# Latent streams of a two-block transformer kernel: a first pass for eight picks, and tile 1's heads between the first value sums

## The chip, the cores and the metric

The kernel runs on one core of one Trainium2 chip. The metric is the device time of one execution in microseconds (us). Before the change it is 2879.14 us, the median of three executions (2868.58 to 2879.42).

## The reference, cut to what matters

Two blocks of two layers each run over 256 positions with 1024 channels, all in float32. The change touches the second block's latent layers. Such a layer mixes (attention with 8 heads over 512 keys, beside a convolution) and then applies `peer`, which picks 16 of 16384 experts per head and position:

```
q = (h @ w_pq).reshape(B, T, PEER_HEADS, 2, PEER_HALF)            # 8 heads, 2 halves
s = jnp.einsum('bthcd,hckd->bthck', q, sub_keys)                  # 128 keys per half
top_s, top_i = lax.top_k(s, PEER_TOPK)                            # 16 of 128, per half
cand = top_s[..., 0, :, None] + top_s[..., 1, None, :]            # 16 x 16 sums
best_s, best_j = lax.top_k(cand.reshape(..., 256), PEER_TOPK)     # 16 of 256
expert = top_i[0][best_j // 16] * PEER_KEYS + top_i[1][best_j % 16]
w = softmax(best_s)
act = gelu(einsum('cd,ced->ce', h, u_tab[expert]))
out = einsum('ce,ced->cd', act * w, v_tab[expert])
```

Each position has its own 128 experts (8 heads of 16), and each expert is one row of u and one of v, 8 KB together.

## The kernel before, in words

The 256 positions are two tiles of 128, one position per partition. The context part and the first block run first, then the two latent layers, one after the other. A latent layer ends in a stream of 256 fetches: fetch n brings, for each of the 128 positions of tile n // 128, the u and v of that position's pick n % 128, which is 1 MB (an indirect DMA that GpSimd issues in `latent_pool`, L2950). Every fetch then goes through four steps in order of n: VectorE multiplies u with h and sums (the dot, L2895); ScalarE takes the gelu (L2835), multiplies with the weight (L2838) and scales an identity by it (L2842); TensorE multiplies that with v and sums over all picks of the tile in PSUM (the value sum, L2756).

The data lands in slots of 8 KB per partition. `ring_plan` gives each fetch the slot that has been unused longest among those that `SLOT_FROM_TO` allows for its n. A slot that has been used waits for the value sum of its last fetch; a slot that is taken for the first time waits for whatever held its memory. `SLOT_QKT` lies on the attention's queries and keys, `SLOT_PROBS` on its probabilities, `SLOT_W0A` and `SLOT_W1A` (from n = 24) on weights that tile 1's last product reads.

The order on each engine is written out by hand. The other work of the layer is hung between the fetches: `latent_mixer_pe`, `latent_mixer_act` and `latent_mixer_dve` each return a table from n to a step. TensorE and ScalarE run the step of n before their part of fetch n, VectorE runs it after the dot of n, and after it the search step of `SEARCH_AT`. A search is `search_keys` (two rounds of eight maxima with their indices over 128 keys, for two halves) and `search_pairs` (the same over 256 sums, then the indices through one-hot sums). The picks of head h are fetches 16 h to 16 h + 15 of their tile; heads 0 and 1 have key scores of their own, and the searches of heads 1, 2 and 3 are hung at n = 1 and 4, 8 and 14, 21 and 27.

Tile 1's attention heads (QH = 8 to 15) have these pieces: a score on TensorE (L802), its maximum on VectorE (L1476), the exponentials on ScalarE (`exps`, L1132), the transposition on TensorE (`turn_probs`, L820), its copy on ScalarE (`probs_turned`, L1140) and the product with the values on TensorE (`sum_values`, L829); at the end `merge_heads` on VectorE (L1498). Before the change TensorE and ScalarE do all of this ahead of fetch 0; VectorE takes two maxima at -2 and two at -1, then two after the dots of 0 and 1, and merges after the dot of 2.

## Time and profile before

| what | value |
|---|---|
| median of three executions | 2879.14 us |
| the profiled execution's own time | 2881.62 us |
| its span, first to last instruction | 2879.7 us |
| TensorE, VectorE, ScalarE, GpSimd busy | 84%, 73%, 28%, 38% of the span |
| 1038.87 MB by DMA, over the span | 361 GB/s |
| dots L2895, mean | 1219 ns |
| value sums L2756 in W slots, mean of one matmul | 627 ns |
| idle before the dots in W slots | 188.1 us, for a DMA |

The profiled execution lies 2.5 us above the median, 1.9 us of it outside the span. The two latent streams lie at about 1393 to 2069 us and 2208 to 2871 us of the span. Busy shares are means over stages with different limits, so the rows further below are of one stage.

### The profile page before, as it was taken

What the parts mean: (1) busy time and instruction counts of PE and PEld (TensorE: products, weight loads), DVE (VectorE), ACT (ScalarE), POOL (GpSimd) and SP (SyncE); (2) the same over time, 40 slices, a digit from 0 to 9 for tenths busy, and PEclk for the clock granted to TensorE, in tenths of its full rate; (3) what the DMA queues carried; (4) which work ended last, traced back from release to release, by engine and by line L of the source; (5) the groups of instructions that cost most, each with busy time, mean ns of one, the idle gap of its engine ahead of it and who ended that gap; (6) DMA issues with size and microseconds to landing.
All of it is one profiled execution on the core that took longest, in us unless ns stands there. A gap on an engine that the chain in (4) does not pass through costs nothing.

```text
span 2879.7 us, 27669 instructions
## 1 busy us (share of the span) xinstructions
PE 2409.2 (84%) x8548; PEld 1374.1 (48%) x8548; DVE 2108.8 (73%) x4518; ACT 816.6 (28%) x2272; POOL 1100.1 (38%) x1090
## 2 busy tenths in 40 slices
PE   6886887989987899988798877869797998877876
PEld 3654464756546566656444333324374444332322
DVE  1869479888878978868787777765475877777654
ACT  1221111000102100013443443334324544433443
POOL 0000444856463676532243333334121434333331
PEclk9897987999986899998999899899998999998999
DMA  8548999999999999963699999999933999999997
GB/s 334 225 164 334 399 413 376 368 412 412 393 407 381 384 398 412 412 259 104 265 398 420 415 420 420 420 419 404 372 124 119 382 420 421 420 421 420 420 420 320
DMA packets 183477, 1038.87 MB, mean 361 GB/s; under 512 B 26971, under 2 KB 28978, under 8 KB 99876
## 3 DMA queue, kind: packets, MB, share of 16 engines
q0 software_dynamic: 147456, 805.37, 69.2%
q1 hardware_dynamic: 35292, 230.38, 20.0%
q8 instruction: 69, 1.13, 0.2%
q10 hardware_dynamic: 584, 1.36, 0.1%
q14 instruction: 76, 0.62, 0.1%
HBM read 1032.60 MB, written 4.44 MB: 360 GB/s over the span
## 4 chain that ended last, share of the span: by engine, by line
DMA 24%; PE 16%; DVE 8%; ACT 3%; issue 2%; POOL 0%; another core or an unknown queue 0%; ACTq 0%; POOLq 0%; DVEq 0%
PE PS L2756 10%; DMA W<-in_peer_uv,IDX 8%; DMA QKT<-in_peer_uv,IDX 7%; DMA MORE<-in_peer_uv,IDX 5%; PE PS L364 4%; DMA KV<-in_peer_uv,IDX 2%; DMA PROJ<-in_peer_uv,IDX 1%; DMA ROWS<-in_peer_uv,IDX 1%; DVE ROWS L1395 1%; DVE W L2895 1%; ACT SCALE L2842 1%; PE PS L829 1%; DVE BJ L1602 1%; DVE BV L1599 0%; DVE QR L1622 0%
## 5 line engine op out<-in xcount | busy, mean ns | idle before, releaser
L2756 PE MATMUL PS<-W,SCALE 128*128 128x512 f32 x1120 | 541.0, 627 | 111.6 <-ACT SCALE L2842 111.5
L2895 DVE CUSTOM_DVE_ANT_0 W<-W,PS 128x1024 f32<-128x1024 f32 x280 | 337.7, 1219 | 189.7 <-DMA W<-in_peer_uv,IDX 188.1
L2950 POOL DMA_INDIRECT W<-in_peer_uv,IDX x280 | 266.6, 952 | 408.6 <-PE PS L2756 356.2
L2756 PEld LDWEIGHTS PS<-W,SCALE 128*128 128x128 f32 x1120 | 215.5, 200 | 420.3 <-issue 419.5
L2585 POOL DMA_INDIRECT ROWS<-in_peer_uv,IDX x159 | 168.3, 1058 | 429.5 <-DVE IDX L1704 240.6
L2178 PE MATMUL PS<-XT,W 128*128 128x256 f32 x1408 | 307.2, 379 | 0.0
L2178 PEld LDWEIGHTS PS<-XT,W 128*128 128x128 f32 x1408 | 267.5, 190 | 44.9 <-issue 9.6
L2835 ACT ACTIVATE DOT<-DOT 128x1 f32<-128x1 f32 x512 | 103.4, 202 | 581.8 <-DVE DOT L2895 568.7
L364 PE MATMUL PS<-W,XT 128*128 128x512 f32 (+2 forms) x576 | 227.5, 555 | 20.7 <-issue 13.6
L364 PE MATMUL PS<-XT,W 128*128 128x128 f32 (+1 forms) x1344 | 221.8, 326 | 3.7 <-ACT XT L1099 3.7
L2842 ACT ACTIVATE SCALE<-C,COEF 128x128 f32<-128x128 f32 x512 | 205.6, 402 | 49.0 <-PE PS L2756 1.9
L364 PEld LDWEIGHTS PS<-XT,W 128*128 128x128 f32 x1344 | 203.4, 196 | 28.6 <-issue 8.2
L364 PEld LDWEIGHTS PS<-W,XT 128*128 128x128 f32 x576 | 110.2, 202 | 135.9 <-issue 124.4
L2377 DVE CUSTOM_DVE_ANT_0 ROWS<-ROWS,PS 128x1024 f32<-128x1024 f32 x118 | 140.0, 1218 | 36.2 <-DMA ROWS<-in_peer_uv,IDX 29.2
L2838 ACT ACTIVATE COEF<-DOT,WGT 128x1 f32<-128x1 f32 x512 | 150.9, 295 | 47.9 <-ACT DOT L2835 0.7
L364 PE MATMUL PS<-W,CT 128*128 128x512 f32 x320 | 154.2, 641 | 9.2 <-ACT CT L1150 4.2
L2188 PE MATMUL PS<-W,PP 128*128 128x512 f32 x192 | 97.8, 669 | 31.7 <-DVE PP L2545 31.7
L1395 DVE SCALAR_TENSOR_TENSOR ROWS<-ROWS,COLC 128x256 f32<-128x256 f32 x300 | 122.8, 480 | 0.4
L2756 PE MATMUL PS<-PROJ,SCALE 128*128 128x512 f32 x176 | 92.4, 651 | 29.9 <-ACT SCALE L2842 29.8
L2390 DVE SCALAR_TENSOR_TENSOR PROD<-ROWS,COEF,PROD 128x1024 f32<-128x1024 f32 x80 | 102.8, 1285 | 14.8 <-issue 4.0
L364 PEld LDWEIGHTS PS<-W,CT 128*128 128x128 f32 x320 | 65.0, 207 | 91.6 <-issue 81.3
L2585 POOL DMA_INDIRECT ROWS<-in_peer_uv,COEF x80 | 88.0, 1100 | 44.7 <-issue 23.2
(421 smaller groups left out, 3945.5 us busy)
## 6 DMA issues: line engine op xcount, KB each, us to landing
W<-in_w_up SPq DMA_DIRECT2D x44, 1024.0 KB
W<-in_w_in SPq DMA_DIRECT2D x21, 2048.0 KB, 11.2
W<-in_w_mod SPq DMA_DIRECT2D x7, 4096.0 KB, 13.5
W<-in_w_down SPq DMA_DIRECT2D x22, 1024.0 KB
W<-in_peer_wq SPq DMA_DIRECT2D x6, 2048.0 KB, 10.0
W<-in_w_o SPq DMA_DIRECT2D x6, 2048.0 KB, 11.2
W<-in_w_out SPq DMA_DIRECT2D x4, 2048.0 KB, 10.5
ROWS<-in_w_mod SPq DMA_DIRECT2D x5, 1024.0 KB, 12.3
```

Source lines behind the costliest of these rows:

```text
L364: ins = nc.tensor.matmul(PS[:, b, cols[0]:cols[1]], lhs(k), rhs(k), start=start and k == 0, stop=stop and k == n_k - 1)
L1395: ins = nc.vector.scalar_tensor_tensor(B["U"][:, g, :], B["PAD"][:, g, k:k + S], tap, B["U"][:, g, :], ALU.mult, ALU.add)
L2178: ins = nc.tensor.matmul(PS[:, 2 * r + half, j * S:(j + 1) * S], up_half(i, half)[:, k, j * P:(j + 1) * P], XT[:, k, :], start=(k == 0), s ...
L2377: nc.vector.tensor_tensor_reduce(beside_slot(l, m), beside_slot(l, m), h, 1.0, 0.0, ALU.mult, ALU.add, DOT[:, 0, m:m + 1]).then_inc(beside ...
L2390: nc.vector.scalar_tensor_tensor(total, slot, coef, total, ALU.mult, ALU.add).then_inc(beside_used, 1)
L2585: nc.gpsimd.indirect_dma_start(beside_slot(l, n), None, one_by_one, bass.IndirectOffsetOnAxis(index[:, n % PICKS:n % PICKS + 1], 0),).then ...
L2756: ins = nc.tensor.matmul(PS[:, SUMS2[t] + h, :], SCALE[:, n % NSCALE, :], v_of(n)[:, h * 512:(h + 1) * 512], start=m == 0, stop=m == PICKS ...
L2835: nc.scalar.activation(DOT[:, t, one], DOT[:, t, one], ACT.Gelu).then_inc(s.gelu_ready, 1)
L2838: nc.scalar.activation(COEF[:, t, one], DOT[:, t, one], ACT.Copy, scale=WGT[:, t, one]).then_inc(s.coef_ready, 1)
L2842: nc.scalar.activation(SCALE[:, n % NSCALE, :], ident, ACT.Copy, scale=COEF[:, t, one]).then_inc(s.scale_ready, 1)
L2895: nc.vector.tensor_tensor_reduce(u_of(n), u_of(n), h_of(t), 1.0, 0.0, ALU.mult, ALU.add, DOT[:, t, m:m + 1]).then_inc(s.rows_used, 1)
L2950: nc.gpsimd.indirect_dma_start(pair_slot(n), None, in_pairs, bass.IndirectOffsetOnAxis(IDX[:, t, m:m + 1], 0),).then_inc(pair_signal(fetch ...
```

## The change

It has four parts.

1. VectorE runs a new `first_picks` ahead of the search of head 0: one round of eight maxima over the keys of each half, the 8 x 8 sums, their eight best, and the indices from them. GpSimd may issue fetches 0 to 7 on its signal. The full search of head 0 follows; it leaves out the first round over the keys, whose result it already has, and signals fetches 8 to 15.
2. Tile 1's heads are hung into the stream. TensorE does only the first two scores ahead of fetch 0, and takes the next pair of scores, two transpositions and two value products ahead of its part of fetches 1, 3, 5 and 7. ScalarE does the first two exponentials and head 0's softmax ahead of fetch 0, and the rest ahead of fetches 1, 3, 5 and 8. VectorE takes two maxima ahead of fetch 0 and two each after the dots of 1, 3 and 5.
3. TensorE's banks for these steps are 0, 1 and 6. What comes behind is shifted: the merge from 2 to 8, the two steps after it from 3 and 7 to 9 and 13, the transposition from 8 to 12 (its copy from 11 to 14), a square root on ScalarE from 4 to 10, the first product from 12 to 15, one copy of queries from 7 to 5 and of scores from 9 to 7. The second product stays at 18.
4. `SLOT_QKT` is allowed from n = 13 and `SLOT_PROBS` from n = 15 (both from 0 before). Fetches 7 to 12 take, again, the slots of fetches 0 to 5.

```diff
-SLOT_FROM_TO = [... (0, 256), (0, 256), (0, 180), (24, 256), ...
+SLOT_FROM_TO = [... (0, 256), (13, 256), (15, 180), (24, 256), ...
@@ latent_mixer_pe
+            banks.banks, banks.i = [0, 1, 6], 0
             score(QH)
             score(QH + 1)
-            for i in range(QH + 2, TT * QH + 2, 2):
+            def more_heads(i):
                 if i < TT * QH:
                     score(i)
                     score(i + 1)
...
-            return {4: lambda: queries(0, 2), 6: lambda: key_scores(0, 2), 8: second_turn, 12: lambda: second_product(0),
+            return {1: lambda: more_heads(QH + 2), 3: lambda: more_heads(QH + 4), 5: lambda: more_heads(QH + 6), 7: lambda: more_heads(QH + 8),
+                    4: lambda: queries(0, 2), 6: lambda: key_scores(0, 2), 12: second_turn, 15: lambda: second_product(0),
@@ latent_mixer_act
+            exps(QH)
+            exps(QH + 1)
+            first_softmax()
+            def more_heads(i):
                 if i < TT * QH:
                     exps(i)
                     exps(i + 1)
+                probs_turned(i - 2)
+                probs_turned(i - 1)
+            def queries_and_heads():
+                queries_in(0, 2)
+                more_heads(QH + 6)
...
-            return {4: lambda: root(act, s, 2, 6, 1.0 / CW2, 1), 7: lambda: queries_in(0, 2), 9: lambda: scores_in(0, 2),
-                    11: lambda: branch_turned("O", 1), ...
+            return {1: lambda: more_heads(QH + 2), 3: lambda: more_heads(QH + 4), 5: queries_and_heads, 7: lambda: scores_in(0, 2),
+                    8: lambda: more_heads(QH + 8), 10: lambda: root(act, s, 2, 6, 1.0 / CW2, 1),
+                    14: lambda: branch_turned("O", 1), ...
@@ latent_mixer_dve
-                -2: lambda: second_maxima(QH), -1: lambda: second_maxima(QH + 2), 0: lambda: second_maxima(QH + 4),
-                1: lambda: second_maxima(QH + 6), 2: second_heads, 3: second_stat, 7: second_ratio, ...
+                -1: lambda: second_maxima(QH), 1: lambda: second_maxima(QH + 2), 3: lambda: second_maxima(QH + 4),
+                5: lambda: second_maxima(QH + 6), 8: second_heads, 9: second_stat, 13: second_ratio, ...
@@ search_for: first_picks, with half = 8
+                for g in range(2): max, then max_index, over the 128 keys
+                tensor_copy of the indices
+                one 8 x 8 tensor_tensor ADD into CAND
+                max and max_index over 64
+                two tensor_scalar (// 8, % 8), one tensor_copy
+                for c in range(2): is_equal; for c: mult; for c: tensor_reduce, each 8 x 8
+                scalar_tensor_tensor, tensor_scalar into IDX[:, 0, 0:8] .then_inc(s.first_picks_ready, 1)
@@ latent_dve
+                    first_picks()
                     search(0, 0)
                     search(0, 1)
-                    later[-2]()
                     later[-1]()
@@ latent_pool
-                        if m % TOPK == 0:
+                        if n == 0:
+                            pool.wait_ge(s.first_picks_ready, 1)
+                        elif n == TOPK // 2 or m % TOPK == 0:
                             pool.wait_ge(s.picks_ready, n // TOPK + 1)
```

## Rows read from the trace of the kernel before

**Rows 1.** Busy time by stretch: us, PE, PEld, DVE, ACT, POOL, PEclk, DMA share, GB/s.
```profile
1400.00:1410.00 10.00, 8.11 (x60) 6.07 (x57) 6.16 (x21) 4.85 (x12) 1.88 (x2) 1.00 1.01 419
1460.00:1470.00 10.00, 10.00 (x25) 4.46 (x24) 9.76 (x23) 3.02 (x10) 6.06 (x6) 1.00 0.95 353
1470.00:1480.00 10.00, 10.00 (x48) 6.42 (x47) 6.95 (x20) 3.90 (x10) 5.33 (x6) 1.00 1.01 419
```
**Rows 2.** Timeline of GpSimd, fetches 0, 7 and 25; the second latent layer's 25.
```profile
1392.75 0.94 POOL L2950 DMA_INDIRECT ROWS<-in_peer_uv,IDX  x1 [24.45 <-DVE EI L1706]
...
1406.86 0.94 POOL L2950 DMA_INDIRECT QKT<-in_peer_uv,IDX  x1 [5.70 <-PE PS L802]
...
1462.30 0.94 POOL L2950 DMA_INDIRECT W<-in_peer_uv,IDX  x1 [6.70 <-PE PS L364]
...
2277.94 0.94 POOL L2950 DMA_INDIRECT W<-in_peer_uv,IDX  x1 [6.68 <-PE PS L364]
```
**Rows 3.** Timeline of VectorE, 1382 to 1476: starts, durations, and every wait.
```profile
1382.60 0.49 DVE L1599 MAX8 TV<-ROWS 128x8 f32<-128x128 f32 x2 [2.77 <-ACT ROWS L1113]
...
1385.82 0.43 DVE L1667 TENSOR_TENSOR QR<-TV 128x256 f32<-128x256 f32 x1
...
1392.25 0.23 DVE L1701 TENSOR_SCALAR IDX<-EI,BASE 128x16 int32<-128x16 f32 x1
...
1394.71 2.49 DVE L1476 TENSOR_REDUCE NMAX<-PS 128x1 f32<-128x512 f32 x4 [2.15 <-PE PS L802]
1398.44 1.22 DVE L2895 CUSTOM_DVE_ANT_0 ROWS<-ROWS,PS 128x1024 f32<-128x1024 f32 x1 [1.24 <-issue]
...
1402.75 1.29 DVE L1476 TENSOR_REDUCE NMAX<-PS 128x1 f32<-128x512 f32 x2 [3.08 <-PE PS L820]
...
1406.58 1.29 DVE L1476 TENSOR_REDUCE NMAX<-PS 128x1 f32<-128x512 f32 x2 [0.92 <-PE PS L802]
...
1412.96 0.20 DVE L1498 RECIPROCAL SUM<-SUM 128x8 f32<-128x8 f32 x1 [0.73 <-PE PS L829]
...
1433.26 0.49 DVE L1599 MAX8 TV<-ROWS 128x8 f32<-128x128 f32 x2 [4.01 <-ACT ROWS L1113]
...
1475.39 1.22 DVE L2895 CUSTOM_DVE_ANT_0 QKT<-QKT,PS 128x1024 f32<-128x1024 f32 x1 [1.53 <-DMA QKT<-in_peer_uv,IDX]
```
**Rows 4.** Timeline of ScalarE: a pair of heads, one fetch's part, a softmax.
```profile
1402.85 1.07 ACT L1140 COPY ROWS<-PS 128x512 f32<-128x512 f32 x2 [3.02 <-PE PS L820]
1403.81 0.70 ACT L1132 ACTIVATE ROWS<-PS,NMAX 128x512 f32<-128x512 f32 x1
...
1412.67 0.20 ACT L2835 ACTIVATE DOT<-DOT 128x1 f32<-128x1 f32 x1
...
1413.60 0.19 ACT L2835 ACTIVATE DOT<-DOT 128x1 f32<-128x1 f32 x1
...
1427.86 0.22 ACT L1228 ACTIVATE EI<-EI 128x16 f32<-128x16 f32 x1
1428.10 1.28 ACT L2835 ACT_TABLE_LOAD   x1
```
**Rows 5.** Timeline of TensorE: heads, value sums, queries; layer 2's first value sum.
```profile
1405.42 1.13 PE L802 MATMUL PS<-QKT 64*128 64x512 f32 x4
1406.48 1.09 PE L820 MATMUL PS<-C,ROWS 128*128 128x128 f32 x8
1407.81 2.00 PE L829 MATMUL PS<-V,ROWS 128*128 128x64 f32 x16 [0.24 <-ACT ROWS L1140]
...
1415.63 1.88 PE L2756 MATMUL PS<-G,SCALE 128*128 128x512 f32 x4
1417.35 1.88 PE L2756 MATMUL PS<-PROJ,SCALE 128*128 128x512 f32 x4
...
1420.78 3.73 PE L364 MATMUL PS<-XT,W 128*128 128x128 f32 x32
...
2229.49 3.52 PE L2756 MATMUL PS<-ROWS,SCALE 128*128 128x512 f32 x4 [0.92 <-ACT SCALE L2842]
```

More of the change, by code:

```diff
@@ L916, in latent_mixer_pe @@
                     sum_values(j)
-            banks.banks, banks.i = [0, 1, 6], 0
             def second_turn():
@@ L1607, in best, with first_picks @@
                         link(ins)
+            def first_picks():
+                half = TOPK // 2
+                keys = B["SC"][0].rearrange("p (g k) -> p g k", k=EK)
+                dve.wait_ge(s.score_read, 2 * heads_up_to(heads, 0, 1))
+                for g in range(2):
+                    ins = nc.vector.max(B["TV"][:, g, 0:half], keys[:, g, :])
+                link(ins)
+                for g in range(2):
+                    ins = nc.vector.max_index(B["TI"][:, g, 0:half], B["TV"][:, g, 0:half], keys[:, g, :])
+                link(ins)
+                nc.vector.tensor_copy(B["TF"][:, 0:2, 0:half], B["TI"][:, 0:2, 0:half])
+                cand = B["CAND"][:, 0:half * half]
+                first = B["TV"][:, 0, 0:half].rearrange("p (k o) -> p k o", o=1)
+                link(nc.vector.tensor_tensor(cand.rearrange("p (a b) -> p a b", b=half), first.to_broadcast([P, half, half]),
+                                             B["TV"][:, 1:2, 0:half].to_broadcast([P, half, half]), ALU.add))
+                bv, bj = B["BV"][:, 0, 0:half], B["BJ"][:, 0, 0:half]
+                link(nc.vector.max(bv, cand))
+                link(nc.vector.max_index(bj, bv, cand))
+                nc.vector.tensor_scalar(B["J"][:, 0, 0:half], bj, 3, None, ALU.logical_shift_right)
+                link(nc.vector.tensor_scalar(B["J"][:, 1, 0:half], bj, half - 1, None, ALU.bitwise_and))
+                link(nc.vector.tensor_copy(B["JF"][:, :, 0:half], B["J"][:, :, 0:half]))
+                hot = [B["HOT"][:, c * half * half:(c + 1) * half * half].rearrange("p (n b) -> p n b", b=half) for c in range(2)]
+                for c in range(2):
+                    ins = nc.vector.tensor_tensor(hot[c], B["JF"][:, c, 0:half].rearrange("p (n o) -> p n o", o=1).to_broadcast([P, half, half]),
+                                                  iota16[:, 0:half].rearrange("p (o k) -> p o k", o=1).to_broadcast([P, half, half]), ALU.is_equal)
+                link(ins)
+                for c in range(2):
+                    ins = nc.vector.tensor_tensor(hot[c], hot[c], B["TF"][:, c:c + 1, 0:half].to_broadcast([P, half, half]), ALU.mult)
+                link(ins)
+                for c in range(2):
+                    ins = nc.vector.tensor_reduce(B["EI"][:, c, 0:half], hot[c], AX, ALU.add)
+                link(ins)
+                link(nc.vector.scalar_tensor_tensor(B["EI"][:, 0, 0:half], B["EI"][:, 0, 0:half], float(EK), B["EI"][:, 1, 0:half], ALU.mult, ALU.add))
+                nc.vector.tensor_scalar(IDX[:, 0, 0:half], B["EI"][:, 0, 0:half], BASE[:, 0:1], None, ALU.add).then_inc(s.first_picks_ready, 1)
@@ L1609, in search_keys @@
             def search_keys(t, h0, h1):
                 dve.wait_ge(s.score_read, 2 * heads_up_to(heads, t, h1))
-                best(B["TV"], B["TI"], B["SC"][t].rearrange("p (g k) -> p g k", k=EK), range(2 * h0, 2 * h1))
+                best(B["TV"], B["TI"], B["SC"][t].rearrange("p (g k) -> p g k", k=EK), range(2 * h0, 2 * h1),
+                     1 if latent and t == 0 and h0 == 0 else 0)
                 link(nc.vector.tensor_copy(B["TF"][:, 2 * h0:2 * h1, :], B["TI"][:, 2 * h0:2 * h1, :]))
```

38 lines of the change are left out of this document (17 added, 21 removed).

## The prediction, made before the changed kernel was run

> **What bounds the kernel now.** I first read the busy time by stretch, because the two latent streams are half of the span. Once a stream runs, its DMA share is 1.01 at 419 GB/s from 1470 us on [rows 1]: that is the limit, 1.0486 MB per fetch, so 2.50 us each. Before that it isn't: from 1460 to 1470 the same columns say 353 GB/s with VectorE at 9.76 of 10 us. The seven stretches of 10 us from 1400 to 1470 moved 26.1 MB (419, 374, 383, 332, 386, 364 and 353 GB/s, of which the first and last stand there) where 419 GB/s would be 29.3, which is 7.7 us lost.
>
> So a stream has a front and a long tail. The tail passes on what the front is late, us for us, since nothing in it can go faster than 2.50 us per fetch. The front must be read from the timelines of the engines. VectorE gets head 0's key scores at 1382.60, puts the indices out at 1392.25, and has its first wait for data in the tail at fetch 27, 1475.39 [rows 3]. GpSimd issues fetch 0 at 1392.75 and fetch 25 at 1462.30, after 6.70 us in which it waits for TensorE's second product (L364), which is hung at n = 18 [rows 2]. With fetch 25 released, the next ones follow at once, since their slots have long been free, and the DMA is full from there. The release of fetch 25 is therefore my point of comparison: what moves it, moves the end. The second latent layer does the same at 2277.94.
>
> How VectorE spends the 80 us up to there is the whole question. Its waits are 2.15, 1.24, 3.08, 0.92, 0.73 and 4.01 us [rows 3], 12.1 us together. All the rest is work.
>
> **The first pass.** It adds, on VectorE's path, one round for two halves: two MAX8 and two index searches. The full search then leaves out just these. By the first row of group 3 two MAX8 take 0.49 us, with the link 0.52, and the whole of head 0's key search ends at 1385.82, after 3.22 us. That is two such rounds, the replacement between them and a cast; I share it out as 1.18 + 0.66 + 1.18 + 0.20. Behind the first round the pass has a cast, an addition, a maximum with its index, two shifts, a cast, three pairs of 8 x 8 operations, a combination and the index itself. An 8 x 8 operation, 64 elements per partition, is not in the trace. From above it is the 0.43 us of the 128x256 addition, from below the 0.20 of the 128x8 reciprocal (the 128x16 index takes 0.23) [rows 3]. By size 64 is nearer to the small ones, so 0.22 us. Sum: 1.18 + 0.20 + 0.25 + 0.59 + 0.29 + 0.21 + 3 x 0.37 + 0.21 + 0.23 = 4.3 us; with 0.43 everywhere 5.9, with 0.20 4.1. Fetch 0 goes out at 1387.1 in place of 1392.75, 5.6 us earlier. VectorE's own search ends 4.3 - 1.2 = 3.1 us later, at 1395.5.
>
> Does the earlier start reach the end? Only if the slots turn over. Fetches 0 to 6 would be landed by about 1408 (1392.8 and six times 2.5). Fetch 7 now needs the slot of fetch 0, so its value sum, and each after it up to 12 the next one's.
>
> **Tile 1's heads, in rounds.** Before, TensorE and ScalarE hand the pairs of heads to each other without a fetch between them. Now every round is a ring: TensorE may not make scores for the round at n before the value sum of n - 1; that needs ScalarE's part of n - 1; ScalarE may not start that before it has done the exponentials of the round before; and these wait for VectorE's maxima, which wait for the scores. VectorE stands in order behind its maxima, so it pays. Durations: two maxima 1.29; an exponential 0.70, and about 0.2 until its sum is out; two copies 1.07; a function table 1.28, needed each time that ScalarE changes between exponential and gelu; ScalarE's part of one fetch 0.95 (1412.67 to 1413.60) [rows 3, 4]; a value sum 1.72 (1415.63 to 1417.35), a score or a pair of transpositions some 0.45 each, queries 3.6 [rows 5]; each hand-over about 0.1.
>
> - Start: VectorE free at 1395.5, two maxima, dot 0 at 1396.8 (landed 1392.8 by the 5.7 us from issue to dot in rows 2 and 3), softmax, dot 1 until 1399.9. ScalarE loads gelu, ends fetch 0's part at 1400.4; its value sum ends at 1402.2; score 10 is there at 1402.8. VectorE waits 2.9, and 0.3 before for the softmax.
> - Round at 1 to round at 3: maximum 10 at 1402.8; exponentials done 1406.0 (the second transposition waits for the first exponential, and frees its buffer); copies 1407.1; gelu table 1408.4; parts of fetches 1 and 2 by 1410.3; two value sums and a score, 1413.4. That is 10.6 us, in which VectorE has 1.3 + 3.2 + 2 x 1.15 = 6.8 of work. It waits 3.8.
> - Round at 3 to round at 5: the same, and the queries (3.6) at n = 4: 14.3 us against 10.4 of work (two maxima, two dots, a search of 6.7 us). It waits 3.9.
> - Round at 5 to the merge at 8: exponentials, copies, table, part of 5 by 1434.2; then head 1's softmax between two table loads, 2.8; part of 6 by 1437.9; value sum 6, transpositions, copies (ScalarE's step at 8), value products, 1443.2. That is 15.5 us against 4.7 of work. It waits 10.8: dots 9 and 10 stand behind the merge, and so do the searches of heads 2 and 3.
> - Behind it about 1.2 for the first product, now at 15.
>
> These are 22.9 us of waits in place of 12.1 [rows 3], so 10.8 more. With the first pass it is 13.9 at VectorE. The dots up to 18 are otherwise the same work; TensorE's product at 18 hangs on them, and by the same steps fetch 25 goes out at 1475.7, 13.4 later than now. I take 13.5 per layer. ScalarE's six extra table loads (7.7 us) are in the rounds already. The shifted small steps (the square root, the second transposition, the ratio) have the next fetches beside them and cost nothing; without that cover, 0.3 to 1.1 us each. `SLOT_QKT` and `SLOT_PROBS` come late, when the rounds have ended, so they take nothing extra.
>
> Both latent layers run this. 2 x 13.5 = 27 us. The profiled execution took 2881.6 us; with the change 2908.6. It lies 2.5 us above the median, so I expect **2906 us** in the runs.
>
> The bounds of the unknown: if half of the rounds' table loads fall into idle time and an 8 x 8 operation takes 0.20, a layer loses 9 (13.5 - 0.2 - 3 x 1.28, and half a us for the sums); with 0.43 and waits a third longer, 21 (13.5 + 1.6 + 5.9). The forecast's own range is 2897 to 2921.
>
> ScalarE's table loads are where a rule speaks harder against the change. In the trace the gelu load starts at 1428.10, 0.02 us after the exponential ended (1427.86 + 0.22), and takes 1.28 [rows 4], and nothing stands around it. The Trainium skill, page "ScalarE: Activation LUTs", section "What ACT_TABLE_LOAD costs", has 1283 ns for the load and some 1380 ns for a drain, about 2.66 us per switch. By the row, six extra loads are 7.7 us per layer; by that rule 16. The row decides, and the drain is not in my sum.
>
> **Rivals.**
> 1. *The early start holds.* Fetches 0 to 7 are there 5.6 us early, the scores are ready when VectorE asks, and the slots turn over in time. For it: VectorE's 12.1 us of waits are there to be filled, and 7.7 us of DMA time are lost before 1470. Then a layer gains 5.6, or 9.5 with half of those: 2870 down to 2862 (median 2868 to 2860). It decides from where VectorE's waits in the front are under 12.1 - 3.1 = 9 us. Against it: nothing in the order lets TensorE make a score before a value sum.
> 2. *It cancels.* The rounds cost, but the DMA, fed earlier and with less queued, catches up; waits of 9 to 13 us. For it: before, GpSimd waits 5.70 us for `SLOT_QKT` at fetch 7 [rows 2]. 2879 to 2886.
> 3. *The clock falls.* TensorE's granted clock is 1.00 throughout 1400 to 1480 [rows 1], the 2.4 GHz level. But the second layer's first value sum takes 3.52 us in place of 1.88, after a wait of 0.92 [rows 5]: the 1.2 GHz level. The rounds leave TensorE waits of 5 us at fetch 0 and some 1.6 within each. If five of the value sums in the rings run at the low level, each 1.6 to 1.7 longer, that is another 8 per layer, 2922.
>
> By the page's rule on the drain (the Trainium skill, as above), another 6 x 1.38 us per layer would be on the ring, by an estimate from its figure 2922 too; the pair of rows cited there shows no drain.
>
> **How the numbers follow.** Forecast 0.65, early start 0.07, cancelling 0.12, clock 0.12, drain 0.04. What a measurement can tell from no change is about 0.5%, 14.4 us: below 2864.7 faster, above 2893.5 slower. Early start is faster in most of its cases: 0.05. Same takes the rest of it, the cancelling and the forecast's edge: 0.15. Slower 0.80. The range is 2880 to 2928: it takes in most of the cancelling and the clock, and leaves the early start and a worse front outside.
>
> **What would show it.** In the profile after: fetch 0 at 1387 (right for the first pass if within 0.5); L1476 with waits of about 3, 4 and 4 us for L802; L1498 with a wait of about 11 for L829; two table loads more at each of the rounds of 1, 3 and 5; fetch 25 at 1476 and no longer at 1462; 419 GB/s behind it as before. The forecast is wrong if fetch 25 is issued before 1466, or if it is late and the stream nevertheless ends as before, which would mean that the tail has reserves.

## The result: slower by 2.3%, over twice the loss that was forecast

The changed kernel takes 2942.62 us, the median of four executions (2937.94 to 2947.37), beside 2875.44 us for the kernel before (2868.58 to 2879.42). The ratio is 1.0226, with a 95% interval of 1.0207 to 1.0246. The forecast was 2906 us with a range to 2928: the sign was right, the size was not. The profiled execution took 2937.94 us, with a span of 2936.1 us, 56.4 more than before. (It lies 4.7 us below its median and the one before 6.2 us above its own, so the traces explain 56 us of a difference of 67.)

I read the trace after as I read the one before. First the release of the fetches by GpSimd (timeline of GpSimd, layer 1; columns: start, duration, the last bracket is its wait and what ended it), against [rows 2]:

```profile
1382.42 0.94 POOL L2999 DMA_INDIRECT ROWS<-in_peer_uv,IDX  x1 [18.76 <-DVE IDX L1652]
...
1399.52 0.94 POOL L2999 DMA_INDIRECT ROWS<-in_peer_uv,IDX  x1 [8.68 <-PE PS L2803]
1413.50 0.94 POOL L2999 DMA_INDIRECT G<-in_peer_uv,IDX  x1 [13.04 <-PE PS L2803]
...
1428.14 0.94 POOL L2999 DMA_INDIRECT KV<-in_peer_uv,IDX  x1 [12.46 <-PE PS L2803]
...
1485.51 0.94 POOL L2999 DMA_INDIRECT W<-in_peer_uv,IDX  x1 [7.89 <-PE PS L364]
```

These are fetches 0, 7, 8, 10 and 25. The first seven start 10.3 us earlier than before on the clock of the trace, but 4.6 of that is only that everything ahead of the stream ended earlier. So I count from t0, VectorE's first MAX8 of head 0 (1382.60 before [rows 3], 1377.95 after). Fetch 0 goes out at +4.5 in place of +10.2. Then fetch 7 needs the slot of fetch 0, and so a value sum, and GpSimd waits 8.68, 13.04 and 12.46 us. Fetch 25 goes out at +107.6 us in layer 1 and +110.1 in layer 2, in place of +79.7 and +80.2. From there to the last dot it takes 599.6 and 590.2 us, before 600.7 and 588.5. The last dots are thus 26.8 and 31.5 us later from t0, together 58.3; with 2.7 more between the streams and 4.6 less ahead of them that is the 56.4 of the span. The whole loss is in the fronts.

The waits of VectorE in layer 1 (its timeline, only starts with a wait of over 1 us, and the first pass's last instruction) answer to [rows 3]:

```profile
1377.95 0.49 DVE L1624 MAX8 TV<-ROWS 128x8 f32<-128x128 f32 x2 [2.77 <-ACT ROWS L1115]
...
1381.91 0.23 DVE L1652 TENSOR_SCALAR IDX<-EI,BASE 128x8 int32<-128x8 f32 x1
...
1401.29 1.29 DVE L1484 TENSOR_REDUCE NMAX<-PS 128x1 f32<-128x512 f32 x2 [6.50 <-PE PS L802]
1415.53 1.29 DVE L1484 TENSOR_REDUCE NMAX<-PS 128x1 f32<-128x512 f32 x2 [7.45 <-PE PS L802]
1434.78 1.29 DVE L1484 TENSOR_REDUCE NMAX<-PS 128x1 f32<-128x512 f32 x2 [9.04 <-PE PS L802]
1452.17 0.20 DVE L1506 RECIPROCAL SUM<-SUM 128x8 f32<-128x8 f32 x1 [12.68 <-PE PS L829]
1476.44 0.75 DVE L1517 SCALAR_TENSOR_TENSOR H<-PS,ri,H 128x512 f32<-128x512 f32 x1 [1.74 <-PE PS L364]
```

The reader is to see that the waits stand where the forecast put them, and that each is longer. Together they are 37.4 us where the forecast had 22.9. In layer 2 they are 40.1. +107.6 less 37.4 is 70.2 us, VectorE's own work up to fetch 25; it is 70.0 in layer 2, and 69.1 to 71.0 in e1 and e4 to e13 below. So in this front fetch 25 is VectorE's work plus VectorE's waits, and each experiment can be read from these two marks. All of these waits end with TensorE; what holds TensorE is in the next view.

One round, from the value sum ahead of the second pair of maxima to the scores of the third, on TensorE and then on ScalarE (timelines):

```profile
1395.50 3.75 PE L2803 MATMUL PS<-ROWS,SCALE 128*128 128x512 f32 x4 [5.07 <-ACT SCALE L2889]
1399.18 2.08 PE L802 MATMUL PS<-QKT 64*128 64x512 f32 x4
1401.19 0.81 PE L820 MATMUL PS<-C,ROWS 128*128 128x128 f32 x4
1404.30 0.63 PE L820 MATMUL PS<-C,ROWS 128*128 128x128 f32 x4 [2.30 <-ACT ROWS L1134]
1406.33 3.68 PE L829 MATMUL PS<-V,ROWS 128*128 128x64 f32 x16 [1.41 <-ACT ROWS L1142]
1409.80 2.93 PE L2803 MATMUL PS<-G,SCALE 128*128 128x512 f32 x4
1412.56 1.88 PE L2803 MATMUL PS<-PROJ,SCALE 128*128 128x512 f32 x4
1414.37 1.13 PE L802 MATMUL PS<-QKT 64*128 64x512 f32 x4
```

```profile
1402.08 1.28 ACT L1134 ACT_TABLE_LOAD   x1 [6.72 <-PE PS L820]
1403.37 0.69 ACT L1134 ACTIVATE ROWS<-PS,NMAX 128x512 f32<-128x512 f32 x1
...
1405.02 0.69 ACT L1134 ACTIVATE ROWS<-PS,NMAX 128x512 f32<-128x512 f32 x1 [0.87 <-PE PS L820]
...
1405.70 1.06 ACT L1142 COPY ROWS<-PS 128x512 f32<-128x512 f32 x2
1406.78 1.28 ACT L2882 ACT_TABLE_LOAD   x1
1408.07 0.20 ACT L2882 ACTIVATE DOT<-DOT 128x1 f32<-128x1 f32 x1
```

This is the forecast's ring, link by link: value sum, score, first transposition, exponential (it overwrites what that transposition reads), second transposition, exponential, copies, value product, value sums, and only then the next scores. Two things in it are longer than [rows 3 to 5] had them. The exponential's table load starts at 1402.08, with the transposition's wait in front of it: it did not happen in the 6.72 us of idling. And the value product takes 3.68 us in place of 2.00, a value sum 3.75 in place of 1.88. The granted clock (busy time by stretch; the columns are as in [rows 1]) says why:

```profile
1390.00:1405.00 15.00, 7.55 (x17) 2.67 (x16) 8.22 (x29) 6.52 (x13) 1.78 (x2) 0.66 0.99 413
1405.00:1420.00 15.00, 10.65 (x36) 6.53 (x36) 7.34 (x19) 7.41 (x16) 1.88 (x2) 0.73 0.33 120
1420.00:1435.00 15.00, 14.32 (x63) 10.26 (x64) 5.59 (x18) 4.46 (x12) 1.88 (x2) 0.70 0.28 96
1435.00:1450.00 15.00, 11.19 (x48) 7.24 (x45) 4.49 (x8) 11.63 (x24) 2.59 (x3) 0.77 0.29 96
```

TensorE was granted 0.66 to 0.77 of 2.4 GHz where it had 1.00 before [rows 1], so half to two thirds of each stretch at the 1.2 GHz level; and the DMA moved 96 to 120 GB/s from 1405 to 1450.

### The profile page after: what moved, and what is told of

Same layout as the page of the kernel before. It is cut to its first block, busy times and chain, and to the rows that moved or that the text cites. A ratio compares the mean times of both kernels' runs of the same rounds, so it can differ in the third digit from the quotient of the medians.

```text
span 2936.1 us, 27715 instructions
## 1 busy us (share of the span) xinstructions
PE 2423.6 (83%) x8548; PEld 1383.4 (47%) x8548; DVE 2113.6 (72%) x4550; ACT 834.8 (28%) x2284; POOL 1105.1 (38%) x1090
## 4 chain that ended last, share of the span: by engine, by line
DMA 22%; PE 18%; DVE 8%; ACT 3%; issue 3%; POOL 0%; ACTq 0%; POOLq 0%; DVEq 0%
DMA W<-in_peer_uv,IDX 12%; PE PS L2803 11%; DMA G<-in_peer_uv,IDX 6%; PE PS L364 4%; DMA ROWS<-in_peer_uv,IDX 2%; DMA PROJ<-in_peer_uv,IDX 2%; DVE ROWS L1403 1%; PE PS L829 1%; DVE W L2942 1%; DMA MORE<-in_peer_uv,IDX 1%; ACT SCALE L2889 1%; DVE BJ L1611 0%; ACT COEF L2885 0%; DVE G L2942 0%; DVE BV L1608 0%
## 5 line engine op out<-in xcount | busy, mean ns | idle before, releaser
L2803 PE MATMUL PS<-W,SCALE 128*128 128x512 f32 x1128 | 551.0, 632 | 110.3 <-ACT SCALE L2889 110.0
L364 PE MATMUL PS<-W,XT 128*128 128x512 f32 (+2 forms) x576 | 218.5, 541 | 15.1 <-issue 7.9
L364 PEld LDWEIGHTS PS<-W,XT 128*128 128x128 f32 x576 | 107.9, 198 | 123.2 <-issue 112.1
L2803 PE MATMUL PS<-PROJ,SCALE 128*128 128x512 f32 x176 | 91.8, 647 | 38.5 <-ACT SCALE L2889 38.5
L2235 PE MATMUL PS<-W,PP 128*128 128x512 f32 x192 | 97.1, 665 | 30.9 <-DVE PP L2592 30.9
L2803 PE MATMUL PS<-MORE,SCALE 128*128 128x512 f32 x176 | 93.6, 658 | 32.8 <-ACT SCALE L2889 32.8
## 6 DMA issues: line engine op xcount, KB each, us to landing
W<-in_w_in SPq DMA_DIRECT2D x21, 2048.0 KB, 12.8
W<-in_w_mod SPq DMA_DIRECT2D x7, 4096.0 KB, 13.6
ROWS<-in_w_mod SPq DMA_DIRECT2D x5, 1024.0 KB, 12.1
```

The source lines that it names most:

```text
L364: ins = nc.tensor.matmul(PS[:, b, cols[0]:cols[1]], lhs(k), rhs(k), start=start and k == 0, stop=stop and k == n_k - 1)
L2803: ins = nc.tensor.matmul(PS[:, SUMS2[t] + h, :], SCALE[:, n % NSCALE, :], v_of(n)[:, h * 512:(h + 1) * 512], start=m == 0, stop=m == PICKS ...
```

## Experiments

Each was profiled; f25 is the start of fetch 25 from t0 in layers 1 and 2, waits is the sum of VectorE's waits of over 0.4 us from t0 to there, clock is TensorE's mean granted clock from 12 us after t0 to there. The time of the kernel before moved between the groups and within them (2869 to 2923 us over all), so a comparison of some us rests on these marks, and the ratios stand beside them. The traces show why: t0 itself lies anywhere from 1377.8 to 1412.1 us, and the stretch from the first stream's last dot to the second t0 takes 133.2 to 143.5 us, and the edits touch neither.

| kernel | f25 | waits | clock | ratio, 95% interval |
|---|---|---|---|---|
| before | +79.7, +80.2 | 12.1, 12.7 | 1.00, 0.97 | 1 |
| after | +107.6, +110.1 | 37.4, 40.1 | 0.80, 0.77 | 1.0226, 1.0207 to 1.0246 |
| e1 first pass alone | +78.9, +78.8 | 8.5, 8.5 | 0.97, 0.97 | 0.9997, 0.9987 to 1.0007 |
| e2 rounds alone | +111.3, +110.2 | 43.8, 42.9 | 0.78, 0.79 | 1.0227, 1.0210 to 1.0244 |
| e3 slots alone | +78.4, +78.6 | 13.2, 12.8 | 0.97, 0.97 | 1.0026, 1.0016 to 1.0035 |
| e4 clock kept | +101.1, +101.0 | 30.9, 31.0 | 0.96, 0.94 | 1.0202, 1.0178 to 1.0227 |
| e5 no tables | +98.2, +102.4 | 27.2, 32.4 | 0.88, 0.81 | 1.0141, 1.0091 to 1.0191 |
| e6 no tables, clock | +102.8, +96.5 | 32.6, 26.5 | 0.89, 0.94 | 1.0138, 1.0088 to 1.0188 |
| e7 merge later | +103.8, +102.0 | 33.8, 32.0 | 0.81, 0.79 | 1.0129, 1.0071 to 1.0187 |
| e8 as e6, fewer fillers | +105.7, +92.9 | 35.5, 22.9 | 0.82, 0.94 | 1.0163, 1.0132 to 1.0195 |
| e9 e8 and e7 together | +92.0, +86.5 | 21.9, 17.3 | 0.91, 0.95 | 1.0096, 1.0070 to 1.0122 |
| e10 scores ahead | +107.9, +108.6 | 37.6, 38.5 | 0.80, 0.81 | 1.0288, 1.0199 to 1.0377 |
| e11 e9, scores ahead | +92.0, +92.3 | 21.6, 22.8 | 0.91, 0.92 | 1.0101, 1.0052 to 1.0150 |
| e12 turned ahead | +97.9, +101.5 | 27.9, 31.7 | 0.84, 0.81 | 1.0170, 1.0145 to 1.0195 |
| e13 e9, turned ahead | +81.0, +81.0 | 11.9, 11.6 | 1.00, 1.00 | 1.0045, 1.0029 to 1.0061 |

### The three parts by themselves: e1, e2, e3

e1 keeps `first_picks` and the halved search, with tile 1's heads and the slots as before; e2 is the change, slots too, without `first_picks`; e3 is the kernel before with one line changed:

```diff
# e2, against the changed kernel
-                    first_picks()
-                        if n == 0:
-                            pool.wait_ge(s.first_picks_ready, 1)
# e3, against the kernel before
-(0, 256), (0, 256), (0, 180), (24, 256)
+(0, 256), (13, 256), (15, 180), (24, 256)
```

> The kernel before with the first pass alone: tile 1's heads stay ahead of the stream and the slots are as before. Theory A (the loss is the rings of tile 1's heads, lengthened by TensorE at its low clock level): the pass puts 3 us of work per layer on VectorE, most of it beside waits for TensorE that were there before; fetch 0 is out about 6 us earlier, fetch 25 within 1 us of before in each layer; the time within 4 us of before. Theory B (the pass itself, 3 us per layer on VectorE's path): 5 to 7 us slower. Theory C (fewer slots starve the stream): same as before, since the slots are as before.

> The changed kernel without the first pass: the search of head 0 is whole, fetch 0 waits for it, all else as changed. Theory A: the changed kernel's time less 0 to 8 us, 2935 to 2943; the waits of VectorE at the rounds stay at 6 to 13 us and TensorE's granted clock at 0.5 in several stretches of 5 us. Theory B: at least 15 us below the changed kernel.

> The kernel before with the slots of the change alone (QKT from fetch 13, PROBS from fetch 15), so fetches 7 to 12 take again the slots of 0 to 5. Theory A: fetch 7 goes out 9 us later, but its dot stood behind a search anyway; 0 to 3 us per layer, 2876 to 2883. Theory C: the seven slots are what starves the front; a third or more of the loss, over 2895.

The rounds, with the slots that go with them, are the whole loss, 1.0227 (2944.5 us, 1.5 above the range expected). The slots alone cost 0.3%, with no loss at fetch 25; that is some 3 us more than was expected of them, and far from the third of the loss that the rival wanted. The first pass gains 0.8 and 1.4 us per layer at fetch 25 and nothing in time. Its fetch 0 is 5.7 us early all the same. Two rows of its GpSimd, fetches 0 and 7, and all waits of over 0.4 us of its VectorE from t0 to fetch 25, layer 1, show where the gain ends:

```profile
1384.39 0.94 POOL L2992 DMA_INDIRECT ROWS<-in_peer_uv,IDX  x1 [18.76 <-DVE IDX L1644]
...
1403.35 0.94 POOL L2992 DMA_INDIRECT QKT<-in_peer_uv,IDX  x1 [10.57 <-PE PS L802]
```

```profile
1398.76 1.29 DVE L1476 TENSOR_REDUCE NMAX<-PS 128x1 f32<-128x512 f32 x2 [2.35 <-PE PS L802]
...
1403.08 1.29 DVE L1476 TENSOR_REDUCE NMAX<-PS 128x1 f32<-128x512 f32 x2 [1.41 <-PE PS L802]
...
1409.46 0.20 DVE L1498 RECIPROCAL SUM<-SUM 128x8 f32<-128x8 f32 x1 [0.73 <-PE PS L829]
...
1429.76 0.49 DVE L1600 MAX8 TV<-ROWS 128x8 f32<-128x128 f32 x2 [4.00 <-ACT ROWS L1113]
```

Fetch 7 waits 10.57 us for `SLOT_QKT`, before 5.70 [rows 2]. But that is not what limits the front: none of the four waits is for a fetch (they are for scores, a value product and key scores), and in e3 fetch 7 goes out 8 us later than before (+32.1 in place of +24.3) with fetch 25 no later. VectorE has 2.8 us more to do and waits 3.6 less. Earlier data could fill only the wait at the dot of fetch 0, 1.24 us in layer 1 [rows 3] and 1.56 in layer 2.

### The clock: e4

```diff
             def more_heads(i):
...
+                fill(7)    # between the two transpositions; 4 behind them, 3 behind the products
+            fill(18)       # ahead of fetch 0; each is a 128*128 by 128x64 product that nobody reads
```

> The changed kernel with small matmuls (64 columns, into a part of a bank that is not yet in use) put where TensorE waits: 18 ahead of fetch 0's value sum, 7, 4 and 3 within each round. Theory A: the granted clock stays near 1.0, value sums take 1.9 in place of 3.7 us, VectorE's four waits fall from 6.5, 7.4, 9.0 and 12.7 us to about 3, 4, 4 and 11, fetch 25 comes 12 to 14 us earlier per layer; 2912 to 2920. If the clock is a by-product and the waits come from the order alone: 2938 or more.

Its busy time by stretch:

```profile
1395.00:1410.00 15.00, 12.71 (x84) 9.28 (x82) 10.80 (x36) 9.26 (x19) 2.50 (x3) 1.00 1.01 412
1410.00:1425.00 15.00, 13.18 (x84) 9.74 (x83) 8.81 (x25) 9.05 (x19) 1.87 (x2) 0.99 0.48 176
1425.00:1440.00 15.00, 13.61 (x76) 9.54 (x76) 7.05 (x15) 4.63 (x10) 1.87 (x2) 0.89 0.40 141
1440.00:1455.00 15.00, 13.13 (x70) 8.37 (x69) 3.02 (x13) 9.31 (x21) 4.12 (x5) 1.00 0.54 193
```

The clock is near 1.00 for most of the front, and 6.5 and 9.1 us of the loss per layer go. Expected were 12 to 14, and waits of about 3, 4, 4 and 11 us; in layer 1 they are 3.75, 5.78, 7.48 and 12.18. So the clock is in the loss, with a quarter to a third of it. What the fillers cost by themselves is inside this number, but it is little: in TensorE's first two rounds of layer 1 each group of fillers is followed by a wait of 0.25 to 0.79 us for something else. (The Trainium skill, "TensorE: Matmul & The Clock Gate", section "HAM oscillation — how this bites in real kernels", tells of a kernel whose clock falls to the lower level time and again because TensorE waits for data inside its loop; these traces agree in kind, with waits for other engines in place of data: 0.66 to 0.77 over 60 us with the waits, 0.89 to 1.00 with them filled.)

### The table loads: e5, e6, e8

```diff
-activation(DOT[:, t, one], DOT[:, t, one], ACT.Gelu)
+activation(DOT[:, t, one], DOT[:, t, one], ACT.Copy if n < 10 else ACT.Gelu)
```

These three, and e9, e11 and e13, leave out the gelu of fetches 0 to 9. e6 has e4's fillers besides, e8 fewer of them (13, 3 and 2).

> The changed kernel with a copy in place of the gelu for fetches 0 to 9 of tile 0 (the gelu is left out there), so ScalarE changes its table no more in the rounds. Theory D (the table loads stand in the ring, both ways: the load for the exponentials waits for TensorE's transposition and so can't run ahead): each round loses two loads, 2.6 us, and the stretch to the merge two more; 8 to 11 us less per layer, 2920 to 2927. Theory E (the loads lie beside other waits, what is left is TensorE's clock and the order): 2938 or more.

> Both at once: no table loads in the rounds (the gelu of fetches 0 to 9 left out) and small matmuls where TensorE waits. If clock and loads are separate costs they add up: 14 to 17 us less per layer than the changed kernel, 2908 to 2915, and what is still above the kernel before is the order itself, 14 to 17 us per layer. If one hides the other: within 5 us of the better of the two alone.

> The changed kernel with two costs taken away together: small filler products on TensorE in the rounds, and a copy in place of the gelu in fetches 0 to 9 (that part of the values is left out), so that ScalarE changes no table inside the rounds. Counted from head 0's first MAX8, fetch 25 goes out at +107.6 and +110.1 us with the change and at +79.7 and +80.2 before. Theory: the clock (6.5 to 9 us) and the tables (8 to 9 us) are separate costs of the ring of the rounds and add up, 14 to 17 us together, so fetch 25 at +92 to +96 in both layers and a time of 2908 to 2916 on a chip where the kernel before takes 2880. Rival, the rounds cost nothing but these two: fetch 25 at +80 to +84, 2880 to 2890. Rival, they hide each other (either alone shows the same slack): +98 to +102.

Without tables 9.4 and 7.7 us go; 8 to 11 were expected. The clock is higher too, 0.88 and 0.81 in place of 0.80 and 0.77, so a part of this may be clock. In layer 2 the two edits together are worth 13.6 (e6) and 17.2 us (e8), where the single ones add up to 16.8 and 14 to 17 were expected. In layer 1 they are worth only 4.8 and 1.9 us, less than the tables alone. The trace of e6 shows what happened (timeline of TensorE, layer 1; L914 is the fillers, 18 products with two records each):

```profile
1428.04 7.94 PE L914 MATMUL PS<-C 128*128 128x64 f32 x36
1435.78 3.73 PE L2813 MATMUL PS<-ROWS,SCALE 128*128 128x512 f32 x4
```

The block of fillers ahead of the first value sum ran at the low level, took 7.94 us, and the value sum followed it without a wait, so here the fillers stood in the way. VectorE's first wait for scores became 9.01 us, in e5 4.99. In e8 the same block took 5.81 us, and TensorE was granted 0.73 from 1400 to 1420. So the two costs add up in layer 2, while layer 1 shows what fillers cost where the clock is already down.

### The merge: e7, e9

```diff
-8: second_heads, 9: second_stat, 13: second_ratio,
+12: second_heads, 13: second_stat, 15: second_ratio,
```

> The changed kernel with VectorE's merge of tile 1's heads after the dot of fetch 12 in place of 8 (the two steps after it at 13 and 15, ScalarE's root at 13), so that dots 9 to 11 and a search fill the wait of 12.7 us. If what stands behind VectorE's in-order wait is what costs: 5 to 7 us less per layer, 2928 to 2933. If TensorE's ring is the limit there too and VectorE's wait only hides it: within 3 us of the changed kernel.

> As the one with fillers and without tables in fetches 0 to 9 (that part of the gelu is left out), and tile 1's merge, variance and ratio at fetches 12, 13 and 15 in place of 8, 9 and 13. In the changed kernel VectorE waits 12.68 us for the value products at the merge. If the rest of the loss, some 14 us per layer, stands at the merge, because dots 9 and 10 and the searches of heads 2 and 3 queue behind it, fetch 25 goes out at +84 to +88. If it is the ring itself (a score may not be made before a value sum, a value sum not before ScalarE's part), the wait only moves to the search that needs the key scores: fetch 25 at +90 to +94, as without this edit, less 1 to 3.

VectorE's wait of 12.68 us for the value products is gone in e7, but the next search waits in its place (timeline of VectorE):

```profile
1461.18 0.49 DVE L1608 MAX8 TV<-ROWS 128x8 f32<-128x128 f32 x2 [9.24 <-ACT ROWS L1115]
```

Net 3.8 and 8.1 us go (expected 5 to 7), and 13.7 and 6.4 on top of the others (e9 against e8; in layer 1 the clock rose with it, from 0.82 to 0.91). e9's +86.5 lies where the theory of the merge had it and its +92.0 where the theory of the ring had it, so this run did not decide between them; the next four go on from there.

### Where the ring closes: e10 to e13

In e9 what is left is the order itself and, in layer 1, some of the low clock (0.91). e10 and e11 put two of the three pairs of scores ahead of a value sum, e12 and e13 the pair and the first transposition of all three rounds:

```diff
+            def scores_of(i):
+                score(i)
+                score(i + 1)
+                turn_probs(i - 2)      # e12 and e13 only
...
+            return {0: lambda: scores_of(QH + 2), 2: lambda: scores_of(QH + 4), ...
```

> The changed kernel with TensorE's scores for the rounds at 1 and 3 issued at 0 and 2, ahead of the value sum of fetch 0 and of fetch 2. In the changed kernel VectorE waits 6.50, 7.45 and 9.04 us for the scores of the three rounds and 12.68 at the merge. Ring theory: the first wait goes (the scores are there before VectorE asks) and the second shrinks by a value sum and ScalarE's part of a fetch, 3 to 5 us, so waits down by 10 in all and fetch 25 at +97 to +101 (from +107.6 and +110.1). Rival, the ring closes over the exponentials and the copies anyway: the waits gained come back at the third round and at the merge, fetch 25 at +104 to +110.

> The same edit on the version with filler products, without the gelu of fetches 0 to 9 (left out of the values) and with the later merge. That one has fetch 25 at +92.0 and +86.5 us, with waits for scores of 5.48, 3.47 and 3.61 us in layer 2. Ring theory: the first goes, the second falls to about 1, the third stays or gains 1: waits of 9 to 11 in place of 17.3, fetch 25 at +79 to +81 in layer 2, about where the kernel before has it (+80.2) though fetch 0 starts 6 us earlier, and a time of 2883 to 2895. Rival, TensorE's and ScalarE's work between the rounds is the bound, whatever the order of the scores: +85 to +87.

> The changed kernel with TensorE's scores and the first of the two transpositions of each of the three rounds issued one fetch earlier, ahead of a value sum. Ring theory (an exponential may not start before the transposition that frees its buffer, and that stood behind a value sum): ScalarE's waits for L820 ahead of an exponential fall from 6 to 8 us to under 2, each round loses 4 to 5 us, part of it comes back at the merge, fetch 25 at +95 to +101 from t0 in place of +107.6 and +110.1, VectorE's waits 26 to 31 us in place of 37.4 and 40.1. Rival, the work of TensorE and ScalarE between the rounds is the bound whatever its order: fetch 25 at +104 to +110 again.

> The same edit on the version with filler products, without the gelu of fetches 0 to 9 (left out of the values) and with the later merge, which has fetch 25 at +92.0 and +86.5 us. Ring theory: the waits of 5.48, 3.47 and 3.61 us for the scores fall under 2 each, fetch 25 at +78 to +81, where the kernel before has it, and 2880 to 2892 us. Rival: +86 to +92.

With the scores alone the expectation fell: in e10's layer 2 the first wait shrinks and the next grow to 11.48 and 9.78 us, and fetch 25 is 0.3 us later and 1.5 us earlier than in the changed kernel, as its rival had it. e11's layer 2 is even 5.8 us later than e9's and outside both expectations; why is open. With the transposition the expectation for fetch 25 held in layer 1 and was missed by 0.5 us in layer 2; of the waits for L820 ahead of a round's exponentials, forecast under 2 us, one is 2.91 and one 5.74. The table loads and exponentials of ScalarE in e12's layer 1, for the rounds at 1 and 3, and the one late load of layer 2:

```profile
1399.34 1.28 ACT L1142 ACT_TABLE_LOAD   x1
1400.63 0.69 ACT L1142 ACTIVATE ROWS<-PS,NMAX 128x512 f32<-128x512 f32 x1
...
1402.93 0.69 ACT L1142 ACTIVATE ROWS<-PS,NMAX 128x512 f32<-128x512 f32 x1 [1.52 <-PE PS L820]
...
1410.84 1.28 ACT L1142 ACT_TABLE_LOAD   x1 [2.91 <-PE PS L820]
...
2248.68 1.28 ACT L1142 ACT_TABLE_LOAD   x1 [5.74 <-PE PS L820]
```

In the changed kernel these loads came after waits of 6.72 and 6.15 us for L820 in layer 1, 6.04 and 7.22 in layer 2. e12 computes all that the changed kernel does and gets 9.7 and 8.6 us back per layer by this order alone. The clock hardly explains it: e10 had 0.80 and 0.81, e12 0.84 and 0.81, and in layer 2, at the same clock, e12's fetch 25 is 7.1 us earlier. The two differ in the transpositions and in the third pair of scores, which e10 leaves behind its value sum; these were not taken apart. With the other costs gone too, e13 has fetch 25 at +81.0 in both layers, within 1.3 us of before, at a clock of 1.00 in both. It has the slots of the change as well, so these hold nothing up at fetch 25. VectorE's waits for scores did not fall under 2 us as expected; in layer 1 they are

```profile
1412.51 1.29 DVE L1502 TENSOR_REDUCE NMAX<-PS 128x1 f32<-128x512 f32 x2 [2.80 <-PE PS L803]
...
1425.68 1.29 DVE L1502 TENSOR_REDUCE NMAX<-PS 128x1 f32<-128x512 f32 x2 [2.95 <-PE PS L803]
...
1435.54 0.49 DVE L1626 MAX8 TV<-ROWS 128x8 f32<-128x128 f32 x2 [5.15 <-ACT ROWS L1133]
```

In layer 2 the steps to fetch 25 are 110.1 (after), 92.9 without tables and with fillers (e8), 86.5 with the later merge (e9), 81.0 with the transposition ahead (e13), and 80.2 before. In layer 1 they are 107.6, 105.7, 92.0, 81.0 and 79.7. Both end where the kernel before is, so no large cost is left out. But the shares differ, 17.2, 6.4 and 5.5 us against 1.9, 13.7 and 11.0, and the clock rose along the way (0.94, 0.95, 1.00 and 0.82, 0.91, 1.00). What each part is worth by itself is thus known only within some us.

### A version meant to beat both: c1, c2, c3

They keep the first pass and the order of before for tile 1's heads, and put other work into VectorE's waits:

```diff
-SEARCH_AT = {1: (1, 0), 4: (1, 1), ...
+SEARCH_AT = {4: (1, 1), ...          # (1, 0) now ahead of the dot of fetch 0
-2: second_heads, 3: second_stat, 7: second_ratio,
+5: second_heads, 6: second_stat, 8: second_ratio,        # c1; the ratio at 13 in c2 and c3
-4: lambda: queries(0, 2), 6: lambda: key_scores(0, 2),
+3: lambda: queries(0, 2), 5: lambda: key_scores(0, 2),
-18: lambda: second_product(1),
+16: lambda: second_product(1),      # c2 and c3 only
```

ScalarE's copies of queries and scores move from 7 and 9 to 4 and 6 and its root from 4 to 7. c3 is c2 with 6, 3 and 2 fillers ahead of the transpositions. Fetch 25 waits for the product that c2 and c3 have at 16, so in these two it stands behind two dots fewer (67.6 to 68.3 us of VectorE's own work in place of 70.2). Their fetch 25 is therefore partly earlier by that alone, and the last dot is the mark to compare.

> A candidate: tile 1's heads ahead of the stream and slots as before, the first pass, and VectorE's waits filled: the key search of head 1 right after dot 0, the merge after dot 5 behind head 1's pairs, queries and scores of heads 2 and 3 one to three fetches earlier. If the front is bound by VectorE's work and waits (12.1 us of waits per layer): 3 to 7 us less per layer, 2866 to 2874 where the kernel before is 2880. If the front is bound by what the DMA brings: no change.

> A version meant to beat both: the order of before for tile 1's heads (one block, no rounds), the first pass in front, head 1's key search put into VectorE's wait for dot 0, the queries and key scores one fetch earlier, tile 1's merge at 5 and 6 and its ratio at 13. Counted from head 0's first MAX8, fetch 25 goes out at +79.7 and +80.2 us before, with VectorE waits of 12.1 and 12.7 us in front of it. If filled waits are worth their length: waits of 5 to 8 us, fetch 25 at +72 to +76, 2867 to 2873 where before takes 2880. If VectorE's work ahead of fetch 25 is the bound and the waits come back elsewhere: +78 to +80, 2878 to 2882. The version tried before this one, with the ratio at 8, had its block of heads at TensorE's 1.2 GHz level in layer 1 (fetch 25 at +93.7) and at 2.4 GHz in layer 2 (+79.2); if that comes again, a layer costs 13 to 15 us more and the time is 2880 to 2896.

> The same version with 6, 3 and 2 small filler products on TensorE ahead of the transpositions in the block of tile 1's heads. If the low clock in that block is a matter of TensorE's short waits in it, the granted clock is 1.00 there in both layers and the block costs the same in both: fetch 25 as in the better layer of the version without fillers, plus at most 1 us. If the clock falls for another reason, both versions show the same.

| kernel | f25 | waits | clock | last dot from t0 | ratio, 95% interval |
|---|---|---|---|---|---|
| before | +79.7, +80.2 | 12.1, 12.7 | 1.00, 0.97 | 680.4, 668.8 | 1 |
| c1 | +93.7, +79.2 | 23.5, 8.8 | 0.79, 0.97 | 692.3, 668.7 | 1.0049, 1.0012 to 1.0086 |
| c2 | +85.8, +75.7 | 17.8, 7.4 | 0.86, 0.97 | 686.6, 667.7 | 1.0028, 1.0001 to 1.0056 |
| c3 | +82.1, +80.4 | 14.4, 12.8 | 0.90, 0.93 | 683.0, 672.3 | 1.0041, 1.0018 to 1.0063 |

None beats the kernel before. c2's layer 2 has the earliest fetch 25 of all, by 4.5 us, and 1.1 us are left of it at the last dot: three of VectorE's dots just before it already wait 1.2 us each for their data, so the DMA, and no longer VectorE, sets the pace there. Its layer 1 missed its range of +72 to +76 by 10 us, at a clock of 0.86. c3's fillers raised the clock in the first layer only in part (0.83 from 1400 to 1420, where c2 had 0.74; fetch 25 is 3.7 us earlier), and in layer 2 its fetch 25 is 4.7 us later than c2's, where at most 1 was expected. In c1 the same order ran at different clocks in the two layers (busy time by stretch, layer 1 and layer 2):

```profile
1400.00:1420.00 20.00, 20.00 (x82) 16.30 (x82) 12.35 (x41) 7.64 (x20) 0.94 (x1) 0.50 0.48 189
1420.00:1440.00 20.00, 20.00 (x83) 12.49 (x81) 11.16 (x29) 9.02 (x25) 5.73 (x6) 0.83 0.66 240
...
2220.00:2240.00 20.00, 17.27 (x113) 12.44 (x110) 18.72 (x56) 14.94 (x38) 2.99 (x4) 1.00 0.85 330
2240.00:2260.00 20.00, 16.56 (x65) 8.62 (x64) 11.36 (x36) 10.82 (x25) 6.26 (x7) 0.91 0.96 361
```

Layer 1's fetch 25 is 14.5 us later than layer 2's.

## Why the prediction was right and wrong

**What bounds the kernel: right.** The tail passed the front's delay on: with fetch 25 27.9 and 29.9 us late, the last dots are 26.8 and 31.5 late. Over all 18 traces the way from fetch 25 to the last dot takes 598.1 to 602.8 us in the first stream and 588.5 to 592.5 in the second.

**The first pass: right to 0.1 us.** It takes 4.2 us to the indices of the first eight (1377.95 to 1382.14), forecast 4.3. The unseen 8 x 8 operation takes 0.22 us, the value taken:

```profile
1379.21 0.22 DVE L1632 TENSOR_TENSOR QR<-TV 128x64 f32<-128x64 f32 x1
```

Fetch 0 starts 4.47 us from t0, forecast 4.5. VectorE's net 3.1 us is 70.2 less the 67.6 that the kernel before has (79.7 less 12.1), so 2.6.

**Tile 1's heads in rounds: right in the mechanism, too small in two terms.** The ring and each of its links stand in the trace; e2 shows that the rounds are the loss, and e12 and e13, which undo a link of the ring, that their order is in it. The step that failed is the length of the ring. The prediction had the first score at 1402.8, which is 20.2 us from t0, then "10.6 us" from the round at 1 to the round at 3, "14.3" to the round at 5 and "15.5" to the merge. Measured, between the rows of VectorE above, these are 23.3, 14.2, 19.3 and 17.4. The four sums miss 3.1, 3.6, 5.0 and 1.9 us, 13.6 of the 14.4 by which fetch 25 is later than forecast (27.9 less 13.5). They miss for two reasons.

- *The exponential's table load.* The prediction let ScalarE load the table while it idled ("exponentials done 1406.0" is 3.2 us behind the maximum). In the trace the load comes behind the transposition's wait, and the same span is 4.5 us (1401.29 to 1405.8). That is 1.28 us in each of three rounds, 3.8. The prediction says that all six extra loads "are in the rounds already", but its steps hold only the three of the gelu. e5 took away both loads of each round, 7.7 us of loading, and got 9.4 and 7.7 us.
- *The clock.* Every TensorE step in the ring was priced at the 2.4 GHz level. The rest of the miss, 9.8 us in layer 1, I put down to value sums, value products and scores at the other level. The trace agrees: up to the merge TensorE's steps in the rings are 12.8 us longer than in [rows 5] (four value sums 6.2, three value products 5.0, scores and queries 1.5), not all of it on the path; e4 got 6.5 and 9.1 us with fillers. Rival 3 had this mechanism, with five value sums and 8 us per layer, and I gave it 0.12 as an alternative to the rings. It was no alternative: the kernel with the rings runs at 0.80 and 0.77, and with their waits filled at 0.96 and 0.94 (e4), so it belonged in the sum. It was the rival's error too to price value sums alone; the value products add 1.7 us each. One price was misread besides: a pair of transpositions takes 1.09 us in [rows 5] and not "some 0.45".

That the merge at 8 would be the largest wait was right (12.68 us; forecast 10.8). That it holds up the searches behind it, as the prediction said, is shown by e7, 4 to 8 us, and by e9.

**The range failed** with this step: it took the clock as an "or", so its end at 2928 held the one or the other. With both terms the sum is 2 x (13.5 + 3.8 + 8) = 50.6 us, on the profiled execution's 2881.6 makes 2932.2, and the profiled execution after took 2937.9.

**The rivals.** The early start did not hold: waits of 37 us, not under 9; and in e1, where they are 8.5 and under the 9 from which that rival was to decide, a layer gains 0.8 and 1.4 us at fetch 25 and not 5.6, since VectorE's waits are for other engines and not for data. It did not cancel either: the waits are 37 us, not 9 to 13. The drain: the load at 1406.78 starts 0.02 us after the copies end (1405.70 + 1.06), takes 1.28 and the gelu follows at 1408.07. The page's rule (the Trainium skill, "ScalarE: Activation LUTs", section "What ACT_TABLE_LOAD costs"), some 1380 ns of drain besides, isn't borne out here; the row decided rightly. Its 1283 ns for the load agree.

**Not in the sum:** the slots. They were said to "take nothing extra"; alone they cost 0.3% (e3), and none of it at fetch 25. In its trace the last dots are 0.8 and 0.0 us later from t0, and of the 7.7 us by which its span is longer 6.1 lie between the streams. So the traces do not put the 0.3% on the slots; where it comes from is open.

**What stays open:** why the clock was up under the fillers in e4 and down in layer 1 of e6, e8 and, in part, c3. And e10's time, 1.0288, is above the changed kernel's with the same marks; in its trace t0 lies 33 us later and the stretch between the streams is 6 us longer, and its interval is wide (1.0199 to 1.0377), so nothing rests on it.

## What to carry to other kernels

When work of three engines that hand it round is hung between the steps of a stream, write the ring out per step and ask which link stands behind a stream step only by the order written on one engine: here one transposition per round, which frees the buffer that the next exponential overwrites, was, with the scores ahead of it, worth 9.7 and 8.6 us per layer, and two of the three pairs of scores without it at most 1.5. Price every TensorE step of such a ring at the lower clock as well, and add that to the sum rather than beside it, since here the kernel with the ring's waits ran at 0.8 of the clock. A faster start is worth only what the engine behind it waits for data: here 1.2 to 1.6 us, and 5.7 us at the first fetch became 0.8 and 1.4.
